# Gate products per head on stacked high and low parts of u, with half-height evictions, in a two-layer diffusion backbone

## What is computed

```python
def block_diag_linear(u, w, b):            # w: (16 heads, 64, 64)
    y = jnp.einsum('bnhd,hde->bnhe', u.reshape(bsz, n, LRU_HEADS, LRU_BLOCK), w)
    return y.reshape(bsz, n, LRU_WIDTH) + b

def rglru_coeffs(u, w_a, b_a, w_x, b_x, lam):
    r = jax.nn.sigmoid(block_diag_linear(u, w_a, b_a))
    i = jax.nn.sigmoid(block_diag_linear(u, w_x, b_x))
    log_a = -LRU_C * r * jax.nn.softplus(-lam)
    a = jnp.exp(log_a)
    return a, jnp.sqrt(-jnp.expm1(2.0 * log_a)) * (i * u)
```

## Time and profile before

| what | value |
| --- | --- |
| median of the runs (2 runs) | 1395.14 us (1394.89 to 1395.39) |
| the profiled execution | 1395.62 us |
| its span, first to last instruction | 1393.8 us |
| mean granted TensorE clock | 0.992 |
| layer 0's eight rounds | about 37 to 612 us of the span |

### The profile page before, as it was taken

The page is one execution under the profiler, slowest core; times in us unless marked ns, Lnnn a source line. Parts: engine busy times, 40 slices in busy tenths (PEclk is TensorE's granted clock), DMA queues, the critical chain, the costliest instruction groups (busy, mean ns, idle before and its releaser), DMA issues. The chain is left out here.

```text
span 1393.8 us, 20353 instructions
## 1 busy us (share of the span) xinstructions
PE 1342.8 (96%) x7116; PEld 1139.1 (82%) x7116; DVE 1017.8 (73%) x1446; ACT 763.6 (55%) x1230; POOL 466.7 (33%) x231
## 2 busy tenths in 40 slices
PE   5999999999999999999999999999998999999998
PEld 4787888888888888877888888878786888888786
DVE  6789969696969696885346457679864899998732
ACT  5465646464646465673122224443344899999421
POOL 0022323232323232312345342013201666667543
PEclk9999999999999999999999999999999999999999
DMA  9323231313131313255675764555699533252694
GB/s 374 150 97 102 79 104 60 103 60 103 60 103 60 103 60 104 62 217 201 198 250 195 235 233 167 196 181 171 192 255 276 191 110 88 83 154 78 184 266 126
DMA packets 107807, 210.29 MB, mean 151 GB/s; under 512 B 11840, under 2 KB 60512, under 8 KB 105440
## 3 DMA queue, kind: packets, MB, share of 16 engines
q1 hardware_dynamic: 107744, 209.48, 46.1%
HBM read 151.76 MB, written 57.69 MB: 150 GB/s over the span
## 5 line engine op out<-in xcount | busy, mean ns | idle before, releaser
L1065 PE MATMUL slab<-h_hi,w_hi 128*128 128x512 f32 x720 | 256.4, 356 | 3.4 <-DVE h_lo L404 2.6
L1066 PE MATMUL slab<-h_lo,w_hi 128*128 128x512 f32 x720 | 255.7, 355 | 0.0
L1067 PE MATMUL slab<-h_hi,w_lo 128*128 128x512 f32 x720 | 255.3, 355 | 0.0
L1037 POOL TENSOR_TENSOR w_lo<-wraw,w_hi 128x1024 fp32r<-128x1024 f32 x29 | 78.3, 2698 | 300.6 <-ACT w_hi L657 300.6
L1065 PEld LDWEIGHTS slab<-h_hi,w_hi 128*128 128x128 f32 x720 | 136.5, 190 | 23.2 <-DVE h_lo L404 2.9
L2894 POOL TENSOR_TENSOR probs<-probs,rdenom 128x2560 f32<-128x2560 f32 (+1 forms) x32 | 135.7, 4242 | 53.0 <-DVE rdenom L2842 53.0
L1067 PEld LDWEIGHTS slab<-h_hi,w_lo 128*128 128x128 f32 x720 | 136.5, 190 | 19.2
L1066 PEld LDWEIGHTS slab<-h_lo,w_hi 128*128 128x128 f32 x720 | 136.6, 190 | 18.9
L2863 DVE TENSOR_TENSOR pt_lo<-TB,pt_hi 128x512 fp32r<-128x512 f32 x152 | 103.8, 686 | 21.8 <-ACT pt_hi L2802 17.2
L2763 ACT ACTIVATE probs<-probs,neg_max 128x640 f32<-128x640 f32 (+1 forms) x128 | 102.7, 802 | 11.7 <-DVE neg_max L2834 9.4
L2834 DVE CUSTOM_DVE_ANT_0 probs<-S,mask,nsink 128x640 f32<-128x640 f32 (+1 forms) x128 | 107.5, 843 | 2.1 <-PE S L2925 2.1
(11 more groups left out here) (411 smaller groups left out, 3503.3 us busy)
## 6 DMA issues: line engine op xcount, KB each, us to landing
wraw<-in_w_in SPq DMA_DIRECT2D x32, 512.0 KB, 3.5
wm<-in_wm SPq DMA_DIRECT2D x32, 512.0 KB, 3.6
early<-in_w_in SPq DMA_DIRECT2D x26, 512.0 KB, 4.0
mixT<-work SPq DMA_DIRECT2D x16, 640.0 KB, 4.0
wm<-in_wm SPq DMA_DIRECT2D x8, 1024.0 KB, 16.0
mraw<-mixT SPq DMA_DIRECT2D x16, 512.0 KB, 7.6
w_sum<-early SPq DMA_DIRECT2D x16, 512.0 KB, 3.4
w_raw<-w_sum SPq DMA_DIRECT2D x16, 512.0 KB, 5.1
```

The lines of the kernel that those rows point to most:

```text
L1037: sub(w_lo[:, j % 2].rearrange("p k n -> p (k n)"), wraw[:, j % 2, :], v32(w_hi[:, j % 2].rearrange("p k n -> p (k n)")), ALU.subtract).th ...
L1065: nc.tensor.matmul(out, l_hi, r_hi, start=start, stop=False)
L1066: nc.tensor.matmul(out, l_hi, r_lo, start=False, stop=False)
L1067: return nc.tensor.matmul(out, l_lo, r_hi, start=False, stop=stop)
```

## The change

The weights of one head are laid out on 64 rows of input by 128 columns (64 of gate a, 64 of gate x; for the second head x comes first), and the DMA writes the same 64 rows into both halves of the partitions. u is split into two tiles, one for each head: `u_parts[head]` has the head's 64 channels' high part on the head's own half of the partitions, and their low part on the other half. One matmul with the high weights then sums over high and low parts at once, a second adds the low weights. A product is now "head and chunk", 2 matmuls instead of 3, and holds both gates of one head on the two halves of a bank. It is read by two ScalarE instructions of 64 partitions, one into A and one into B. The order of TensorE's stages stays.

Beside this: the u high part is two ScalarE copies of 64 partitions, the low part two VectorE subtractions instead of one on GpSimd; modulation sum 0 moves behind the convolution (in round 0 it stays); in rounds 1 to 7 the three tanh of slab GF are spread: chunk 0 behind the d = 0 gates, chunk 1 between y's high part and the root, chunk 2 behind the root; in rounds 1 to 6 the tanh of G's chunk 0, and in all rounds the high parts of the Fourier products and of the next weights, are put between L686 and L692 of d = 1 (`between`; round 0 had the Fourier high part there already), and G's chunks 1 and 2 ahead of the second root. The matching VectorE steps move too. The diff, cut:

```diff
-        u_hi, u_lo = sb("u_hi", [P, T], F32R), sb("u_lo", [P, T], F32R)
+        u_parts = [sb("u_parts0", [P, T], F32R), sb("u_parts1", [P, T], F32R)]
+        HALF = (slice(0, HEAD), slice(HEAD, P))
...
-                for c in range(2):
-                    sp.dma_start(gw[HEAD * c:HEAD * (c + 1), :, HEAD * c:HEAD * (c + 1)],
-                                 a["w_gate"][t, HEAD * c:HEAD * (c + 1), :, :]).then_inc(gw_ld, 16)
+                for rows in HALF:
+                    sp.dma_start(gw[rows], a["w_gate"][t]).then_inc(gw_ld, 16)
...
             def gates(t, d, first, between=None):
...
+                for head in range(2):
+                    to = HALF[head]
                     for c, (at, n) in enumerate(CHUNKS):
-                        k = 6 * d + 3 * x + c
+                        k = 6 * d + 3 * head + c
                         act.wait_ge(gp_, 12 * t + k + 1)
-                        nc.scalar.activation(dst[:, at:at + n], W[:, k % 4, 0:n], ACT.Tanh, scale=0.5,
-                                             bias=cur[:, C_HALF + 2 * x + d:C_HALF + 2 * x + d + 1]).then_inc(gr, 1)
-                act.wait_ge(gr, 12 * t + 6 * d + 3)
+                        for x, dst in enumerate((A, B)):
+                            col = C_HALF + 2 * x + d
+                            nc.scalar.activation(dst[to, at:at + n], W[HALF[head ^ x], k % 4, 0:n], ACT.Tanh, scale=0.5,
+                                                 bias=cur[to, col:col + 1]).then_inc(gr, 1)
+                act.wait_ge(gr, 24 * t + 12 * d + 12)
...
-                nc.scalar.activation(u_hi[:], u[:], ACT.Copy).then_inc(uh, 1)
+                for head, rows in enumerate(HALF):
+                    nc.scalar.activation(u_parts[head][rows], u[rows], ACT.Copy).then_inc(uh, 1)
...
                 gates(t, 0, first)
                 if not first:
+                    silu_gf(t, False, (0,))
                     split_hi(t, SLAB_G)
                 act.wait_ge(yr, t + 1)
...
                 nc.scalar.activation(y_hi, xf[:], ACT.Copy).then_inc(yh, 1)
+                if not first:
+                    silu_gf(t, False, (1,))
                 root(t, 0)
                 if first:
                     tanh_g(t, (0, 1))
                 else:
-                    silu_gf(t, False)
+                    silu_gf(t, False, (2,))
...
-                if first:
-                    gates(t, 1, True, pq_high)
-                else:
-                    gates(t, 1, False)
+                def between():
+                    if not first and not last:
+                        tanh_g(t, (0,))
                     pq_high()
-                if last:
-                    mixed_hi(0, 0)
-                else:
-                    split_hi(t + 1, SLAB_U)
+                    if last:
+                        mixed_hi(0, 0)
+                    else:
+                        split_hi(t + 1, SLAB_U)
+
+                gates(t, 1, first, between)
+                if not first and not last:
+                    tanh_g(t, (1, 2))
                 root(t, 1)
...
                 if first:
                     dve.wait_ge(sbd, 2)
-                mod_sums(t, 0, E)
-                if first:
+                    mod_sums(t, 0, E)
                     mod_sums(t, 1, E)
...
                     silu_gf(0)
                 dve.wait_ge(conv, 2 * t + 2)
                 if not first:
+                    mod_sums(t, 0, E)
+                for head, rows in enumerate(HALF):
+                    dve.wait_ge(uh, 2 * t + head + 1)
+                    nc.vector.tensor_tensor(u_parts[head][HALF[1 - head]], u[rows], v32(u_parts[head][rows]),
+                                            ALU.subtract).then_inc(ul, 1)
...
                 direction(0)
+                if not first:
+                    silu_gf(0)
                 dve.wait_ge(yh, t + 1)
                 tt(y_lo, xf[:], v32(y_hi), ALU.subtract).then_inc(yl, 1)
+                if not first:
+                    silu_gf(1)
                 scan(0)
...
-                pool.wait_ge(uh, t + 1)
-                sub(u_lo[:], u[:], v32(u_hi[:]), ALU.subtract).then_inc(ul, 1)
...
-            def gate_products(t, d):
-                for x in range(2):
-                    for c, (at, n) in enumerate(CHUNKS):
-                        k = 6 * d + 3 * x + c
-                        if k < 3:
-                            pe.wait_ge(xr, 3 * t + k + 1)
-                        elif k > 3:
-                            pe.wait_ge(gr, 12 * t + k - 3)
-                        mm3(W[:, k % 4, 0:n], gw_hi[:, 2 * d + x, :], gw_lo[:, 2 * d + x, :],
-                            u_hi[:, at:at + n], u_lo[:, at:at + n], True, True).then_inc(gp_, 1)
+            def gate_products(t, d, products=range(6)):
+                for i in products:
+                    head, c = i // 3, i % 3
+                    at, n = CHUNKS[c]
+                    k = 6 * d + i
+                    if k in (0, 3):
+                        pe.wait_ge(ul, 2 * t + head + 1)
+                    if k < 3:
+                        pe.wait_ge(xr, 3 * t + k + 1)
+                    elif k > 3:
+                        pe.wait_ge(gr, 24 * t + 2 * (k - 3))
+                    out, parts = W[:, k % 4, 0:n], u_parts[head][:, at:at + n]
+                    nc.tensor.matmul(out, gw_hi[:, 2 * d + head, :], parts, start=True, stop=False)
+                    nc.tensor.matmul(out, gw_lo[:, 2 * d + head, :], parts, start=False, stop=True).then_inc(gp_, 1)
...
                     if i % 2 == 0:
-                        pe.wait_ge(gr, 12 * t + 9 + i // 2)
+                        pe.wait_ge(gr, 24 * t + 2 * (9 + i // 2))
```

More of the change, by code:

```diff
@@ L707, in f_tokens, with silu_gf @@
                     nc.scalar.activation(xf[:, at:at + n], W[:, c, 0:n], ACT.Copy).then_inc(xr, 1)
-            def silu_gf(t, first):
+            def silu_gf(t, first, chunks):
                 if first:
@@ L713, in silu_gf @@
                     act.wait_ge(mf, t)
-                for c, (at, n) in enumerate(CHUNKS):
+                for c in chunks:
+                    at, n = CHUNKS[c]
                     act.wait_ge(s_gf, 3 * t + c + 1)
@@ L808, in body @@
                     weight_hi(2)
-                else:
-                    tanh_g(t, (2,) if first else range(3))
+                elif first:
+                    tanh_g(t, (2,))
                 act.wait_ge(uv, t + 1)
@@ L967, in body @@
                 else:
-                    for c in range(3):
-                        silu_gf(c)
+                    silu_gf(2)
                 direction(1)
-                if not first:
-                    dve.wait_ge(om, 2 * t + 2)
-                    mod_sums(t, 3, E)
+                if not first and not last:
+                    silu_g(0)
                 dve.wait_ge(pqh, t + 1)
                 tt(pq_lo[:], Wf[:, 0:PQ_N], v32(pq_hi[:]), ALU.subtract).then_inc(pql, 1)
-                if first:
-                    dve.wait_ge(om, 2 * t + 2)
-                    mod_sums(t, 3, E)
+                if not first and not last:
+                    silu_g(1)
+                dve.wait_ge(om, 2 * t + 2)
+                mod_sums(t, 3, E)
+                if not first and not last:
+                    silu_g(2)
                 scan(1)
@@ L987, in body @@
                     weight_lo(2)
-                else:
-                    for c in (2,) if first else range(3):
-                        silu_g(c)
+                elif first:
+                    silu_g(2)
                 dve.wait_ge(us, t + 1)
@@ L1172, in body @@
                     slab_product(t, SLAB_G, True, (0, 1))
+                    gate_products(t, 1)
                 else:
                     slab_product(t, SLAB_GF, False)
-                gate_products(t, 1)
+                    gate_products(t, 1)
                 dft_product(t)
@@ L3333 @@
     w0 = slabs(g["l0_w_in"])
-    w_gate = np.stack([g["l0_w_a"][0], g["l0_w_x"][0], g["l0_w_a"][1], g["l0_w_x"][1]])
+    wa, wx = (g["l0_w_" + n].reshape(2, KT, 2, HEAD, HEAD) for n in "ax")
+    w_gate = np.stack([np.concatenate([(wa, wx)[h], (wx, wa)[h]], -1)[:, :, h] for h in range(2)], 1)
     w1, kv = g["l1_w_in"], N_KV * HEAD
```

38 lines of the change are left out of this document (15 added, 23 removed).

## The result

The changed kernel takes 1465.6 us (1465.06 to 1466.14, two runs). Its time over that of the kernel before is 1.0508 (95% interval 1.0483 to 1.0534): 5.1% slower, 70.5 us. The forecast was 1442 us, with a range up to 1458. The direction was right; the loss was half as large again as forecast.

What follows compares the result with a forecast made beforehand. Taken as TensorE-bound, with the second gates at risk of waiting for the scan. Seven rounds at +5.7 us (+39.9) and round 0 at +7.3 sum to +47.2: 1442 us, 3.4% slower, range 1417 to 1458.

Steps and rivals of the forecast that it cites:

- What bounds the kernel, and where it would break: TensorE-bound; at the second gates the scan is in time by under 0.2 us, so the fifth product would wait 4.9.
- Twelve take 6.2 us: Half readings of a gate stage on ScalarE: each costs what a whole one costs, 3.1 us more in each stage.
- Then comes the tanh of GF's chunk 1, which waits for TensorE: ScalarE ahead of the root: this tanh waits until TensorE delivers at 307.3; the first second-gates reading comes 3.8 us later.
- I take 0.6: Behind the second gates' gap: TensorE's clock falls for 3.3 us, partly hidden, adding 0.6 us per steady round.
- The bound of 1.6: Upper limit of the clock's cost per round, if no part of the 3.3 us low stretch is hidden.
- 5.7 forecast: Lengthening of a steady round in us: 5.1 from the late scan and paced readings, 0.6 from the clock.
- 7.3 forecast: Lengthening of round 0 in us: gates start at 94.2 instead of 91.96, next slab at 129.3 against 121.99.
- Seven rounds (1 to 7): All rounds after round 0, the last included, charged the same 5.7 us each: +39.9 us.
- TensorE's saving: Gate stages fall from 18 to 12 matmuls, 2.35 us each, saving 2.3 a round, but the waits take it away.
- The move of u's low part to VectorE, and the round's end: Two subtractions fit nearly free in steady rounds; the round's end comes about 1 us before the next convolution; nothing charged.
- Half-price readings: Rival on ScalarE's gate readings: half a whole's cost each, +17 to +29 us, 1412 to 1424 us; chance 0.11.
- A second wait at the round's end: Rival: second root behind slab G's last tanh, overrunning the next gates by 2 us a round, 1456 us; chance 0.10.

Runs made afterwards that it cites:

- Run 2: Kernel before the change, with only each gate product read by two ScalarE instructions of 64 partitions added: 1453.21 us, ratio 1.0413.
- run 5: Changed kernel with the two half readings of every second product in swapped order, so neighbours across products read the same partitions: 1458.73 us, ratio 1.0461.
- run 1: Changed kernel with one whole reading over 128 partitions per gate product, six a stage, the two gates left unsorted: 1433.46 us, ratio 1.0271.
- run 3: Changed kernel's stacked products and half readings, with ScalarE's and VectorE's other steps in the order from before the change: 1454.67 us, ratio 1.0423.
- run 4: Changed kernel with 42 unread matmuls ahead of the fifth product of the second gates in rounds 1 to 7: 1462.96 us, ratio 1.0476.
- run 8: Changed kernel with whole readings (gates unsorted) and slab G's chunk 0 in the gap of the second gates: 1393.39 us, ratio 0.9986.
- run 6: Changed kernel with slab G's chunk 0 moved between the fourth and fifth product of the second gates, rounds 1 to 7: 1426.97 us, ratio 1.0244.

## Why the prediction was right in sign and short in size

- **What bounds the kernel, and where it would break: right.** The wait stands at the fifth product of the second gates, behind the scan, in every round: 5.4 us in the steady ones, 4.9 forecast.
- **"Twelve take 6.2 us": this step failed.** The bound from above was taken as "a half costs what a whole costs", and it does in duration (0.69); but the step of whole ones, 0.58, was carried over too. Measured are 0.71 for 512 columns and 0.50 for 256. The upper bound of the unseen operation left out that its overlap with the neighbour might go, though the earlier trace rows have both numbers, duration and step. Runs 2 and 5 show the change of partitions as what takes the overlap away. It enters twice: 1.4 us more ahead of the scan, and 1.4 us in the readings that pace the Fourier products.
- **"Then comes the tanh of GF's chunk 1, which waits for TensorE": did not happen.** ScalarE came to it at 332.48, 11.4 us after slab GF began at 321.06, and the chunks were done. With readings at 6.2 us a wait of 0.7 would have stood there; run 1, with shorter ones, has it (0.87). The readings end 1.4 us later than forecast and L683 starts another 0.2 later; of these 1.6 only 0.9 reach the scan (3.8 forecast, 4.7 measured), since the 0.7 of waiting falls away. That the two tanh ahead of the root lengthen the chain was right: run 3 gives 1.15 us a round for both.
- **"I take 0.6" for the clock: too small by half.** The stretch was 6.4 us, not 3.3, and by run 4 it costs 1.2 us a round. The bound of 1.6 held. The duration of the low clock in layer 1 was read behind a gap with dense work after it; here the matmuls behind the gap were spaced by the readings. Run 1, whose readings space them less, had 2.9 to 4.2 us behind gaps of up to 5.9. But run 5, with slightly shorter readings, had up to 7.9, so what sets the length is not shown.
- **Their sum.** 5.7 forecast, and 0.9 ahead of the scan, about 1.2 in the paced stretch and 0.7 for the clock: 8.5, against 8.6 measured. The whole miss is 23.6 us (70.8 of the span, 47.2 forecast). Rounds 1 to 6 give 15.6 of it. Round 0 gives 2.1 (9.4, 7.3 forecast: gates at 93.01 instead of 94.2, but the fifth product and the last products 0.8 and 2.0 later than forecast, by the longer readings).
- **"Seven rounds (1 to 7)" at one price: a term was missing for the last.** It gives the other 5.9 us (11.6, 5.7 forecast). The forecast put nothing for the table load of 1.28 us that the new order brings ahead of its first readings, nor for the wait of 1.83 us and the 3.1 us of low clock that follow. Its second gates have a low clock of 8.2 us as well, longer than the 6.8 us at most of rounds 1 to 6.
- **TensorE's saving: right that it is lost.** The first gates took 4.19 us (3.74 forecast), so the stage is even longer than before. The saving itself was put too high: without the halves a stage takes 2.57 to 2.63 us (run 8), not 2.35, so 1.9 a round instead of 2.3.
- **The move of u's low part to VectorE, and the round's end: right that they are free.** No TensorE wait names the two subtractions in steady rounds. The first tap waits 0.58 us for VectorE's L871 in steady rounds: the slack of 1 us was used up, and TensorE did not wait for it.
- **The rivals.** Half-price readings: out, by the rows. A second wait at the round's end: its figure, 1456, was nearer than the forecast, but the mechanism is not there. The range went up to readings of 0.6 us each, and they took 0.64 on average (7.64 over twelve); with the clock and the last round erring the same way, the time fell outside it.

The Trainium skill (ScalarE: Activation LUTs, What ACT_TABLE_LOAD costs) states that back-to-back ACTIVATEs overlap by about 93 ns. The trace agrees for whole tiles (0.58 to 0.59 us apart with 0.69 each, six in 3.16 us) and where partitions stay the same (0.58 apart, run 5), and not where they change (0.71 apart).

## What to carry to other kernels

Splitting an eviction (the reading of a finished product out of PSUM) by partitions saved nothing on ScalarE here and cost twice: each half has the whole's duration (0.69 us for 64x512 as for 128x512), and in addition the overlap with the neighbour is lost where the partitions alternate. Before TensorE's share of a stage is cut, look for what reads its products: here a third of the gate matmuls went, and the stage became longer, because the reader became the bound. When a wait opens in TensorE's program, independent work moved into it (run 6: 6.6 us a round) is worth far more than a restored order (1.15) or filler (at most 1.2); count the ends of the loop by themselves, since there the gain was given back, and look for a table load that a new order puts on the path of the first or the last round.

## What the runs showed of the hardware beyond that

- ScalarE's overlap of about 0.1 us between neighbouring activations vanishes when the partitions read or written change from one to the next: 7.64 us for twelve, 7.09 with four of the eleven changes removed, and 6.2 by the steps of whole ones. Run 2 has the same 7.63 with tile and bias column unchanged inside a product.
- The low clock behind a gap is not a fixed price. Behind 5.4 us of gap and with spaced matmuls it lasted 6.4 us here, behind 5.9 us of gap and with whole readings 3.4 (run 1, the same round), and 7.2 to 7.9 in three rounds of run 5. What sets the length is open. A gap filled with 42 unread matmuls kept the clock in some rounds and not in others, though the matmuls were the same in all.
